# Two modulated norms folded into their products: token factor on the results, shift as spare columns

## The reference, cut to what matters

```
def _rmsnorm(x, g):
    y = x * lax.rsqrt(jnp.mean(x * x, axis=-1, keepdims=True) + EPS)
    return y * g
def _modulate(h, shift, scale):
    return h * (1 + scale) + shift
# norm 4: hn  = _modulate(_rmsnorm(x, norm1_g), shift1, scale1);  hn @ w_in   (2816 columns)
# norm 5: the same of the 256 context tokens, with the context's shift and scale
# norm 6: hn2 = _modulate(_rmsnorm(x, norm2_g), shift2, scale2);  relu(hn2 @ w_ff1)**2 @ w_ff2
```

## Time and profile before

| what | value |
|---|---|
| time of three runs, median (lowest to highest) | 2621.13 us (2620.13 to 2621.93) |
| span of the profiled execution, first to last instruction | 2614.0 us |
| what the median of the runs has above that span | 7.1 us |
| TensorE busy | 2485.6 us, 95% of the span |
| VectorE, ScalarE, GpSimd busy | 53%, 32%, 10% |
| mean granted TensorE clock | 0.960 of full speed |

### The profile page before, as it was taken

How to read it: one execution, slowest core, us unless ns; L and a number is a source line. 1 busy time by engine, 2 the same in 40 slices (tenths; PEclk the granted TensorE clock), 3 DMA queues, 4 the chain that set the end, 5 groups by cost and what they waited for, 6 DMA issues and landing times.

```text
span 2614.0 us, 38591 instructions
## 1 busy us (share of the span) xinstructions
PE 2485.6 (95%) x15967; PEld 2186.3 (84%) x15967; DVE 1387.1 (53%) x1904; ACT 834.1 (32%) x1197; POOL 265.5 (10%) x203
## 2 busy tenths in 40 slices
PE   6999999999999999999989999998997899899998
PEld 6999999998999999999887888886884446688886
DVE  6677555655544344542665666677117563534433
ACT  4433444434322122321324222223223453322322
POOL 2000222223100000200111000002003101000001
PEclk9999999989999999999869999998997899899999
DMA  3222433335222222222002544451320001122221
GB/s 133 81 74 78 125 82 89 86 73 189 81 98 81 97 82 94 98 81 81 33 1 97 193 146 159 161 188 56 118 81 17 0 1 45 59 92 97 94 97 65
DMA packets 93871, 235.47 MB, mean 90 GB/s; under 512 B 60074, under 2 KB 61700, under 8 KB 69556
## 3 DMA queue, kind: packets, MB, share of 16 engines
q1 hardware_dynamic: 88208, 201.40, 23.9%
q10 hardware_dynamic: 5540, 32.30, 3.6%
HBM read 222.00 MB, written 11.67 MB: 89 GB/s over the span
## 4 chain that ended last, share of the span: by engine, by line
PE 88%; DVE 7%; ACT 2%; issue 1%; DMA 1%; POOL 0%; DVEq 0%; ACTq 0%; POOLq 0%; SPq 0%
PE ps L298 68%; PE ps L1086 1%; PE ps L1076 1%; PE ps L302 1%; PE ps L1100 1%; PE ps L2563 1%; PE ps L2581 1%; PE ps L1878 1%; PE ps L2571 1%; PE ps L1879 1%; PE ps L1113 1%; PE ps L1112 1%; PE ps L1118 1%; DVE g_tmp L1300 1%; PE ps L1034 1%
## 5 line engine op out<-in xcount | busy, mean ns | idle before, releaser
L298 PE MATMUL ps<-xa_hi,whi 128*128 128x264 f32 (+1 forms) x2512 | 655.2, 320 | 44.7 <-DVE wlo L321 20.1
L298 PE MATMUL ps<-xa_lo,whi 128*128 128x264 f32 (+1 forms) x2512 | 649.9, 318 | 0.0
L298 PE MATMUL ps<-xa_hi,wlo 128*128 128x264 f32 (+1 forms) x2512 | 648.4, 317 | 0.0
L321 DVE TENSOR_TENSOR wlo<-raw,whi 128x2048 fp32r<-128x2048 f32 x161 | 370.1, 2299 | 255.2 <-ACT whi L314 252.5
L298 PEld LDWEIGHTS ps<-xa_hi,whi 128*128 128x128 f32 x2512 | 417.7, 190 | 88.2 <-DVE wlo L321 22.2
L314 ACT ACTIVATE whi<-raw 128x2048 fp32r<-128x2048 f32 x161 | 307.5, 1910 | 570.2 <-PE ps L298 561.2
L298 PEld LDWEIGHTS ps<-xa_hi,wlo 128*128 128x128 f32 x2512 | 416.8, 190 | 30.2
L298 PEld LDWEIGHTS ps<-xa_lo,whi 128*128 128x128 f32 x2512 | 416.9, 190 | 30.0
L298 PE MATMUL ps<-xb_lo,whi 128*128 128x264 f32 (+1 forms) x1280 | 384.5, 341 | 0.0
L298 PE MATMUL ps<-xb_hi,whi 128*128 128x264 f32 (+1 forms) x1280 | 382.5, 339 | 1.5 <-DVEq L243 1.5
L298 PE MATMUL ps<-xb_hi,wlo 128*128 128x264 f32 (+1 forms) x1280 | 382.9, 340 | 0.0
(11 more groups left out here) (424 smaller groups left out, 2811.9 us busy)
## 6 DMA issues: line engine op xcount, KB each, us to landing
raw<-weights SPq DMA_DIRECT2D x161, 1024.0 KB, 4.8
mod_w<-weights_mod ACTq DMA_DIRECT2D x24, 1024.0 KB, 4.8
g_EC<-scr_g SPq DMA_DIRECT2D x10, 424.0 KB, 5.1
scr_z<-z_st SPq DMA_DIRECT2D x16, 264.0 KB, 4.5
g_D<-scr_g SPq DMA_DIRECT2D x10, 371.0 KB, 4.8
scr_a<-g_AT SPq DMA_DIRECT2D x10, 318.0 KB
h<-x_in ACTq DMA_DIRECT2D x4, 528.0 KB, 8.6
z_b<-scr_z SPq DMA_DIRECT2D x1, 2112.0 KB
```

Source lines behind the costliest of these rows:

```text
L298: mm = pe.matmul(ps[:, at_ + step * c + bank, 0:tn], w[:, hb.slot, k, c * P:(c + 1) * P], x[:, k, t0:t0 + tn], start=(k == 0 and n == 0), ...
L321: dve.tensor_tensor(wlo[:, hb.slot], raw[:, hb.raw_slot], whi[:, hb.slot].bitcast(F32), ALU.subtract).then_inc(S("w_lo"), 1)
```

## The change

Norm turns 4 and 6 become folded turns too. `xa_hi` and `xa_lo` hold gain * h in columns 16 to 527, made behind each tile of h, and in columns 12 to 15 (`SHIFT_COLS`, four equal copies) the shift, in the same two parts. The products of `b2_in` and of the up half of MLP2 run over 516 columns, as two pieces of 258 (`SHIFTED`), so columns 12 to 15 of a result are shift @ w. `rstd` is 1 in those columns. As a result leaves PSUM, DVE multiplies all 516 columns by `rstd` into an SBUF tile (`b2_y`, or `m_act` in MLP2), and ACT adds one of the four columns as its bias: Identity or Silu into the output in `b2_in`, Relu into `m_y` in MLP2. In MLP2 the square is then taken twice, by ACT (rounded, into `xb_hi`) and by DVE (exact, into `m_act`), and DVE subtracts.

Three more things go with it. The modulation's first half (shift1 and scale1, and the context's) gets its bias in the middle of each group instead of at its end, and the gains and the shift's copies of norm 4 are made before the last down half of MLP1. The context's products move from the odd bank of each pair to banks 6 and 7, with a semaphore of their own. And several semaphores of earlier stages are merged under one name with offsets, which changes no instruction there.

```
+        SH = (SEQ + 4) // 2
+        SHIFTED = [(0, N_META - 4, SH), (1, N_META - 4 + SH, SH)]
+        SHIFT_COLS = slice(N_META - 4, N_META)
...
                             ehi, elo, en = extra
-                            mm = pe.matmul(ps[:, 2 * c + 1, 0:en], w[:, hb.slot, k, c * P:(c + 1) * P],
+                            mm = pe.matmul(ps[:, 6 + c, 0:en], w[:, hb.slot, k, c * P:(c + 1) * P],
...
-        RAW_TURNS = [0, 1, 2, 3]
+        RAW_TURNS = [0, 1, 2, 3, 4, 6]
+        def act_shift_high(act, what):
+            x = shift_of(what)
+            a, b = x.shape[1], x.shape[2]
+            act.activation(xa_hi[:, :, SHIFT_COLS].rearrange("p (a b) t -> p a b t", b=b), x[:, :, :, None].to_broadcast([P, a, b, 4]), ACT.Copy)\
+                .then_inc(S("shift_hi"), 1)
+        def dve_shift_low(dve, what, n):
...
+            dve.wait_ge(S("shift_hi"), n + 1)
...
# act_two_layers
+                        if biased:
                             act.wait_ge(S("two_ev"), i * 16 + (16 * base + t + 3))
+                            act.activation(flat(m_y[:, c], pieces), flat(m_act[:, c], pieces), func, bias=m_act[:, c, N_META - 1:N_META])\
+                                .then_inc(S("two_act"), 1)
+                            act.wait_ge(S("two_act"), i * 8 + (8 * base + t + 1))
+                            act.activation(flat(xb_hi[:, t], pieces), flat(m_y[:, c], pieces), ACT.Square).then_inc(S("two_hi"), 1)
# dve_two_layers
+                        if biased:
+                            dve.wait_ge(S("two_lo"), i * 8 + (8 * base + t + 1))
+                            dve.wait_ge(S("tiles_done"), hb.index * 2 + (t + 1))
+                            dve.tensor_tensor(cols(m_act[:, c], SHIFTED), pair(c, SHIFTED), cols(rstd, SHIFTED), ALU.mult).then_inc(S("two_ev"), 1)
                             dve.wait_ge(S("two_act"), i * 8 + (8 * base + t + 1))
+                            dve.tensor_tensor(flat(m_act[:, c], pieces), flat(m_y[:, c], pieces), flat(m_y[:, c], pieces), ALU.mult)\
+                                .then_inc(S("two_sq"), 1)
...
+                            dve.tensor_tensor(flat(xb_lo[:, t], pieces), flat(m_act[:, c], pieces),
+                                              flat(xb_hi[:, t], pieces).bitcast(F32), ALU.subtract).then_inc(S("two_lo"), 1)
# dve_mod_sums
-            if j == 7:
+            if j in (3, 7):
...
+                    if isinstance(i, int) and i == MOD_GROUPS - 1:
+                        dve_gains(dve, range(0, 2), 3 * MOD_GROUPS - 1)
+                        dve_shift_low(dve, "shift1", 0)
# pe_b2_in
-            pe_hb(pe, HalfBlock(HB_B2_IN), xa_hi, xa_lo, LATE, "in_ev", N_IN_BEFORE, per_k=("norm_lo", 4 * KT))
+            pe.wait_ge(S("shift_lo"), 1)
+            pe_hb(pe, HalfBlock(HB_B2_IN), xa_hi, xa_lo, SHIFTED, "in_ev", N_IN_BEFORE, per_k=("norm_lo", 4 * KT),
+                  freed=lambda c: pe.wait_ge(S("two_ev"), 16 * 10 + 1 + c),
+                  between=lambda: pe_norm_sums(pe, 4, LATE), during=((1, KT // 2), lambda: pe_norm_rows(pe, 4, LATE)))
             pe_norm(pe, 5, CTXP, sq=ctx_sq, to=5)
# act_b2_in
-                act.activation(to, ps[:, 2 * (t % 2), :], func, scale=scale).then_inc(S("in_ev"), 1)
+                act.wait_ge(S("in_ev"), N_IN_BEFORE + 2 + t + 1)
+                act.activation(to, b2_y[:, t % 2, 4:4 + SEQ], func, bias=b2_y[:, t % 2, 3:4]).then_inc(S("b2_out"), 1)
+        def dve_b2_in(dve, first, last):
+            for t in range(first, last):
+                dve.wait_ge(S("tiles_done"), HB_B2_IN * 2 + t + 1)
+                if t >= 2:
+                    dve.wait_ge(S("b2_out"), t - 1)
+                dve.scalar_tensor_tensor(b2_y[:, t % 2, :].rearrange("p (a b) -> p a b", b=SH), pair(t % 2, SHIFTED), P ** -0.5 if t < 4 else 1.0,
+                                         cols(rstd, SHIFTED), ALU.mult, ALU.mult).then_inc(S("in_ev"), 1)
+                if t % 2 and t < 2 * N_B2_IN - 1:
+                    dve_split(dve, HalfBlock(HB_B2_IN + t // 2 + 2))
...
# the engines' programs
-                         dve_norm(dve, 4, 4, 0, h, LATE, lambda k: gain_col(0, k),
-                                  shift=(lambda k: mod_col("shift1", k), 0), split=HalfBlock(HB_B2_IN + 1)),
-                         dve_norm(dve, 5, 5, 1, b_ctx, CTXP, lambda k: gain_col(1, k), shift=(ctx_shift, 1), dst=(bc_hi, bc_lo), at_=5),
-                         dve_b2_in(dve)),
+                         dve_b2_rows(dve),
+                         dve_b2_in(dve, 0, 2),
+                         dve_norm(dve, 5, 5, 0, b_ctx, CTXP, lambda k: gain_col(1, k), shift=(ctx_shift, 0), dst=(bc_hi, bc_lo), at_=5),
+                         dve_b2_in(dve, 2, 2 * N_B2_IN)),
...
-                         pe_norm(pe, 4, LATE),
                          pe_b2_in(pe)),
...
-                         pe_norm(pe, 6, LATE),
-                         pe_two_layers(pe, 10, HB_MLP2, 4, LATE, norm=6, peel=True),
+                         pe.wait_ge(S("shift_lo"), 2),
+                         pe_two_layers(pe, 10, HB_MLP2, 4, LATE, norm=6, peel=True, sums=6, squared=("out_ev", 2 * KT + 2), up=SHIFTED),
```

More of the change, by code:

```diff
@@ L535, in dve_headnorm, with shift_of, pe_two_layers @@
                                              ALU.mult, ALU.mult).then_inc(S("head_out"), 1)
-        RAW_TURNS = [0, 1, 2, 3]
+        RAW_TURNS = [0, 1, 2, 3, 4, 6]
+        def shift_of(what):
+            x = mod_tiles(what)
+            return x if len(x.shape) == 3 and x.shape[1] > 1 else x.rearrange("p a b -> p (a b)")[:, None, :]
+        def act_shift_high(act, what):
[4 more added lines that the diff above has]
+        def dve_shift_low(dve, what, n):
+            x = shift_of(what)
+            a, b = x.shape[1], x.shape[2]
+            dve.wait_ge(S("shift_hi"), n + 1)
+            dve.tensor_tensor(xa_lo[:, :, SHIFT_COLS].rearrange("p (a b) t -> p a b t", b=b), x[:, :, :, None].to_broadcast([P, a, b, 4]),
+                              xa_hi[:, :, SHIFT_COLS].rearrange("p (a b) t -> p a b t", b=b).bitcast(F32), ALU.subtract).then_inc(S("shift_lo"), 1)
         def after_group(n):
             return ("two_ev", 16 * n - KT + 2)
-        def pe_two_layers(pe, base, first, groups, pieces, norm, peel=False, sums=None, squared=None):
+        def pe_two_layers(pe, base, first, groups, pieces, norm, peel=False, sums=None, squared=None, up=None):
             def group(i, hb, start=False):
@@ L550, in group @@
                                    during=((1, KT // 2), lambda: pe_norm_rows(pe, sums, pieces))) if start and j == 0 else {}
-                    pe_hb(pe, hb.after(j), xa_hi, xa_lo, pieces, "two_ev", i * 16 + (16 * base + 2 * j),
+                    pe_hb(pe, hb.after(j), xa_hi, xa_lo, up or pieces, "two_ev", i * 16 + (16 * base + 2 * j),
                           per_k=("norm_lo", norm * KT) if j == 0 else None, **opening)
@@ L575, in act_down, with act_two_layers @@
                     step(j)
-        def act_two_layers(act, base, first, groups, pieces, func, turn, beside=None, rows=None, scaled=None):
+        def act_two_layers(act, base, first, groups, pieces, func, turn, beside=None, rows=None, scaled=None, opening=None, biased=False):
             def group(i, hb, last=False):
@@ L605, in act_two_layers, with dve_two_layers @@
             group(groups - 1, HalfBlock(first + 8 * (groups - 1)), last=True)
-        def dve_two_layers(dve, base, first, groups, pieces, scale=None, beside=None, rows=None, scaled=None):
+        def dve_two_layers(dve, base, first, groups, pieces, scale=None, beside=None, rows=None, scaled=None, biased=False):
             if rows is not None:
@@ L2804, in _ @@
                 lambda: (act_b2_out(act),
-                         act_norm(act, 6, 6, 2, LATE),
-                         act_two_layers(act, 10, HB_MLP2, 4, LATE, ACT.Relu, 7),
+                         act_two_layers(act, 10, HB_MLP2, 4, LATE, ACT.Relu, 7, rows=6, biased=True),
                          act_norm_stats(act, 7, LATE)),
@@ L2841, in _ @@
                 lambda: (dve_b2_out(dve),
-                         dve_norm(dve, 6, 6, 2, h, LATE, lambda k: gain_col(2, k),
-                                  shift=(lambda k: mod_col("shift2", k), 2), split=HalfBlock(HB_MLP2 + 1)),
-                         dve_two_layers(dve, 10, HB_MLP2, 4, LATE, scale=lambda k: mod_col("gate2", k)),
+                         dve_two_layers(dve, 10, HB_MLP2, 4, LATE, scale=lambda k: mod_col("gate2", k), rows=6, biased=True),
                          dve_final(dve)),
```

167 lines of the change are left out of this document (94 added, 73 removed).

## The result

The changed kernel took 2597.4 us (median of 4 runs, 2593.45 to 2603.41) against 2621.53 for the kernel before (4 runs, 2620.13 to 2631.41) beside it: ratio 0.9898, interval 0.9875 to 0.992. Later series of the same two kernels gave 0.9932 (0.9908 to 0.9956) and 0.9934 (0.9913 to 0.9956), both outside the interval of the first four runs. All runs together have their mean at 2620.5 for before (76 runs, standard deviation 5.2) and at 2602.0 for after (19 runs, 6.3): 18.5 us, with an interval of 15.4 to 21.6 worked out from these deviations. The direction and the mechanism were right, the size of 17.0 is inside that interval, and the time by the first ratio was not in my range.

A forecast was written before the change was run, and what follows sets the result against it. TensorE, busy 95%, was taken as the bound. Norm 4 -11.5, norm 6 -16.6, 24 other half blocks +10.3 and projection's end +0.8 gave -17.0: span 2597.0, plus 7.1, 2604.1 us; range 2597 to 2613.

The forecast's parts named there:

- B: Products in two pieces: the second matmul costs little beside its columns, 1.7 to 5 ns a step; middle 2596.8 us, chance 0.10.
- C: Norm 4: DVE is late, lows hold up h by 2 us per half block, context chain slips; 2612.6 us, chance 0.13.
- A step of two 258s: Projection and MLP2's up half: 240.7 ns a step, 9.0 more than now, 11.7 us over 1296 steps.
- Norm 6: Start of MLP2: first half block takes 14.9 us in place of 31.5, a gain of 16.6.
- MLP2: Up half: DVE's third instruction per tile stays hidden, 9.0 us of work and waits in a half block of 11.55.
- D: No gain: a wait for shift or roots holds PE as long as now at one norm; 2620 us, chance 0.04.
- E: Slower: MLP2's longer chain per tile through DVE and ACT bounds its up half blocks; 2627.3 us, chance 0.04.
- Norm 4 and the context: From MLP1's end to the context half blocks: 35.7 us against 48.7, one PE pause left at the context's norm.
- DVE in MLP1's last down half: Added lows and mod sums fill DVE to 11.7 us per half block of 11.12; 1.5 us lost in all.
- The projection's end: Last tile of the projection goes through DVE before ACT, with the stage's end behind it: +0.8 us.
- My term of 11.5: Norm 4 and the context's norm: net gain of 11.5 us, 13.0 less 1.5 lost by DVE.
- the gain of 13.0: Norm 4 to the context half blocks: 13.0 us gained, before the 1.5 lost by DVE in MLP1.

The follow-up runs named there:

- merged names: The kernel before with only the change's merged and renamed semaphores, norms and products as before; 2620.26 us (11 runs), ratio 0.9993.
- squares first: Changed kernel with the third projection half block's weight split behind the context's norm and ACT's context squares ahead of norm 4's root; 2601.76 us (4 runs).

## Why the prediction came out as it did

**The step that failed is the range, "the middle of B at the lower end, C at the upper, 2597 to 2613".** It was made from the prices of the rivals alone, and the scatter from one execution to the next stood in it at nothing. The first four runs of the changed kernel have their median 4.6 us under the mean of all 19. I had a size for such scatter in hand: the prediction puts what one measurement tells from no change at 5.2 us, but used it only for the border between faster and same. With it in the range, 2597 as a lower end was too high.

The sign of it was in the sum, where I misread it: "The median of the runs is 7.1 above the span: 2604.1". I took the 7.1 for something that lies around every execution. A run here is its span plus 1.8 us (2599.2 and 2597.4 for the changed kernel, and 1.7 to 1.9 in every run with both numbers). The remaining 5.3 was scatter: the profiled execution had taken about 2615.8, an estimate from its span and the 1.8, and the three runs shown, within 1.8 us of each other, looked like a kernel that hardly scatters. 76 runs reach from 2610.88 to 2631.92. The forecast itself was not harmed (17.0 off the median of before gives the same 2604.1).

The rest is chance. Of the four runs of before in the first series one, 2631.41, is the second highest of the 76. Four runs drawn at random from the 19 and four from the 76 put the time under 2597 in about one draw in ten (7% by their means, 13% by their medians, an estimate).

**What scatters goes with TensorE's clock.** Over 60 runs of before, time and mean granted clock (0.953 to 0.962) are correlated at -0.92, 2.2 us for each 0.001; over the 19 of after at -0.98 (0.959 to 0.968, 2.35 us). The largest single move lies just ahead of MLP1, from split 79 to 83 (all that comes before split 79 moves as much in sum, 1246.1 to 1259.1 us). The twelve profiles have it in three groups, 157.2 to 158.1 us, 161.6 to 161.7 and 169.2 to 169.7, at a granted clock of 0.85, 0.83 and 0.78. One row of each, first before, then merged names:

```profile
1263.23:1424.85 161.62, 151.67 (x952) 131.19 (x952) 102.07 (x126) 47.13 (x75) 26.63 (x25) 0.83 0.11 40
```

```profile
1264.46:1433.77 169.31, 160.84 (x952) 139.19 (x951) 101.87 (x126) 47.22 (x75) 27.02 (x25) 0.78 0.11 38
```

The same 952 matmuls, 7.7 us apart, and not by waiting: PE stands still for 9.9 us in the one and 8.5 in the other. The three groups don't follow the kernels; before was in two of them, and so was the changed kernel. Inside, a group of 16 small ones takes 1.40 us in the one and 2.70 in the other, windows at 1.00 and 0.50, the 2.4 and the 1.2 GHz level:

```profile
1281.48:1282.88 1.40, 1.40 (x17) 1.40 (x17) 0.76 (x2) 1.40 (x4) 1.28 (x3) 1.00 0.00 0
```

```profile
1282.84:1285.54 2.70, 2.70 (x16) 2.70 (x16) 0.09 (x1) 1.40 (x2) 2.50 (x4) 0.50 0.00 0
```

**Term by term.**
- A step of two 258s: 240.7 ns said, 240.4 in the first tile of the projection; 9.0 ns over one of 512 said, 8.75 found, 7.3 beside the context. Right; the 11.7 us for all of them were 10.8.
- Norm 6: 16.6 said, 31.5 - 15.4 = 16.1 found. Right; the idle time is 0.89 for 0.79, and the first tile 6.01 for 5.78. In the second profile of before this stage (split 129 to 133) is 2.1 us shorter, and the granted clock in the 40 us from the norm's start is 0.79 in place of 0.70, so the gain is not the same in each execution.
- MLP2: no wait of PE after the 0.89 us at its start, up to the last norm. Rivals D and E did not happen. From split 133 to 160 5.3 us were given back, 0.42 for each of some 13 up half blocks.
- Norm 4 and the context: 35.7 said up to the context half blocks, 34.5 found. The pause is as foretold (6.4 said, 1805.60 - 1799.44 = 6.16), in its place and by its chain, and the half block behind it takes 12.93 - 11.8 = 1.1 more at a granted clock of 0.90 (1.2 said; 11.8 is its 49 steps at 240.7). Wrong was that PE would start 1.0 late: it started with no gap.
- DVE in MLP1's last down half: 11.7 of 11.12 us said, 1.5 lost; found 11.13 with 0.53 of it waiting, nothing lost. The mod sums were the error. I put 1.65 each, half of them beside POOL; they come after POOL's sums and take 1.21 each. The lows alone bear POOL, 3.48 a pair as I said. What I had not seen is that POOL too depends on what stands beside it: its two sums take 5.11 us beside the mod sums and 3.96 beside the lows (1766.17 to 1770.13, the mod sums from 1770.60). Rival C dies with that.
- The projection's end: +0.8 said. From split 125 to 126, with the end in it, there are 20.6 us before and in the kernel with merged names, and 20.7 after; nothing to be seen.
- One reading of before was half wrong. I laid the 12.25 us of its second half block to a lower clock. PE's 48 matmuls are 1.2 us slower there, from first to last start 12.19 us against 10.98 in the kernel with merged names, at 1.00. But that cost nothing, since PE stands still behind them in both, for an evacuation by ACT (PE's timelines, before, then merged names):

```profile
1831.47 0.51 PE L298 MATMUL ps<-xa_hi,whi 128*128 128x512 f32 x1 [0.68 <-ACT b_q L2260]
```

```profile
1837.35 0.50 PE L298 MATMUL ps<-xa_hi,whi 128*128 128x512 f32 x1 [1.77 <-ACT b_q L2262]
```

In ACT's row this evacuation comes behind its last rounding for DVE's chain of the context's norm and six DMA issues, 3.1 us. In the changed kernel DVE empties that bank at 1816.76, ahead of ACT's issues, and PE has no such wait. There the lower clock does count, and so the 1.2 that I carried over came true for another reason.
- 48.7 us up to the context half blocks is not what before usually needs: 45.8 in its second profile (1796.84 to 1842.62). The low clock of that one execution had put some 3 us on it. My term of 11.5 is right against the usual case (45.8 - 34.5 = 11.3) and 2.7 short against the profile that I worked from.

The sum from stages, against the second profile of before: 8.7 from split 114 to 123, less 0.9 to 126, 12.6 at norm 6 (64.1 - 51.5; 14.7 against the other profiles), less 5.3: 15.1 to 17.2. From MLP1's first matmul to the end the difference of those two kernels is 1188.7 - 1171.4 = 17.3 us; the 2.6 of it that lie in split 126 to 129 are not the change's, for nothing was edited there, and in MLP1 it loses 0.4. The 17.0 was right in size. That norm 4 came out at 11.3 for my 11.5 is luck: the gain of 13.0 was 1.7 above that of the usual case, the 1.5 for DVE was never lost, and the two errors cancel. What stays open is what sets off the lower clock in one execution and not in the next. All that the runs show is that it differs with the same instructions. That the clock makes the time is shown where the same matmuls take longer at the lower level, as in the rows above; for the whole program it is a correlation.

## What to carry to other kernels

Before a time is forecast to a few us, find out what one execution may differ from the next: a profile's own time beside its span, its granted clock beside that of the other runs. Three runs that agree don't show it; and a stretch in which the clock is below 1 is a place where the profile before you may not be the usual case. To judge a change smaller than that scatter, compare the stages of the traces between two instructions that both kernels have: where the clock was full that gave 0.1 us, and the times gave 3. Counting DVE's round instruction by instruction works, if each is priced by whether GpSimd runs at that very moment.

## What the runs showed of the hardware

Two-input work of DVE is slowed by GpSimd unequally. One low (a SCALAR_TENSOR_TENSOR of 512 columns) takes 0.75 us alone and 1.78 beside POOL. A mod sum of 1024 columns takes 1.22 alone, 1.75 beside POOL's sums of 256 columns (squares first) and up to 2.32 beside its sums of 512 columns (before). The weight split (TENSOR_TENSOR, 2048 columns) took 2.29 in the median of its 161 rows in before, 2.28 also where it lay wholly within POOL's work (at 328.94), and 2.88 at the most (at 17.22, beside POOL). GpSimd is slowed in its turn: the same two sums of 512 columns took 5.11 us beside mod sums and 3.96 beside lows.
